# Stick-breaking suffix sums as two fp32r products in place of one fp32 product, in a one-core decoder layer

## The chip, the cores and the metric

The kernel runs on one core of a Trainium2 chip as a single launch. The metric is device time in microseconds (us) of that core. The engines are TensorE (PE, with its weight loads shown apart as PEld), VectorE (DVE), ScalarE (ACT), GpSimd (POOL) and SyncE (SP, which only issues transfers here). Each runs its own list of instructions in order and waits for the others only at semaphores.

## The reference

One decoder layer over 512 tokens of width 1024. The part that matters here is stick-breaking attention, 8 heads of width 64:

```python
z = einsum(q, k) * dh ** -0.5
before = s_pos < t_pos
log_1m = where(before, log_sigmoid(-z), 0)        # = -softplus(z)
csum = cumsum(log_1m, axis=-1)
log_a = log_sigmoid(z) + (csum[..., -1:] - csum)  # a suffix sum over the keys
a = where(before, exp(log_a), 0)
out = a @ v
```

Around it the layer has a combined input projection, a sparse attention whose indexer picks the 128 best keys per query, a gated merge, an output projection, a router, and 16 SwiGLU experts.

## The kernel before

Phases follow one another on PE: input projections (to about 176 us of the profile), stick-breaking attention (to about 288), sparse attention (to about 370), merge and output projection (to about 475), router, experts.

**Stick-breaking steps.** Heads go in 4 pairs (`hp`), key tiles of 128 from the last to the first (`i` = 3, 2, 1, 0). This gives 16 steps `m`, and step `m` handles for two heads the columns `S - 128 i` of all queries at or after key tile `i`: 128, 256, 384, 512 columns per head, so tiles of 256, 512, 768 and 1024 elements per partition. Keys lie on the partitions. A step is made of:

- `z(m)` on PE (L750): the logits into one of two PSUM tiles `zt`, used in turn. It waits until `weights(m - 2)` has read that tile.
- `soft(m)` on ACT (L1203 to L1205): three passes, Abs, Exp, Ln, that leave log(1 + exp(-|z|)).
- `softplus(m)` on DVE (L1566, L1568): adds max(z, 0) and zeroes what isn't `before`.
- `suffix(m)` on PE (L768, L770): adds minus the softplus tiles of this and all later key tiles to `zt`, by products with `negtri` (own tile) and `negones` (later tiles), both 128x128 fp32, then a bf16 product that masks. One step has (4 - i) such fp32 products for each of two heads; 80 in all.
- `weights(m)` on ACT (L1212): Exp of `zt`, the attention weights `ab`.
- `av_a(hp)` on PE (L783), once per pair: weights times values.

**The order.** In turn `m` of the loop PE issues two "triples" of a gate projection (a triple is three fp32r products of 512 columns, L612 to L614, for an fp32 product split in high and low parts), then `z(m+1)`, the index products of the sparse attention (L796), two more triples, at `i` = 3 also `av_a`, then `suffix(m)`. ACT issues `soft(m+1)`, the relu of the index products (L1189), in even turns the copy of a finished gate block (L1227) and after every second of them the rounding of a weight chunk (L1087), then `weights(m)`. DVE issues `softplus(m+1)`, the score sums (L1590, L1592), at turns 4, 8 and 12 the low part of a weight chunk (L1445), then rounds of the top-k search (`topk_rounds`; one round is L1605 and L1606 on a score row). There are 48 rounds, 16 for each of three query tiles with rows of 256, 384 and 512 elements: four rounds a turn at turns 4 to 7, three a turn from turn 8, and the remaining 8 in the sparse phase.

**Sparse phase.** There are 16 units `p`, four for each query tile. DVE takes `rows(p+1)` (L1653), `normal(p)` (L1665), at p = 1, 5, 9, 13 the low part of a weight chunk, then `topk_rounds(2)` as long as rounds remain. PE's `turn(p)` (L868) waits for `normal(p)`. The mask of the third query tile is needed at unit 8, that of the fourth at unit 12.

Of the kernel before, what the change touches and what calls it, by code (L numbers as in the profile page):

```python
# [19 lines left out]
F32 = mybir.dt.float32  # L20
F32R = mybir.dt.float32r
BF16 = mybir.dt.bfloat16
I32 = mybir.dt.int32
ALU = mybir.AluOpType
ACT = mybir.ActivationFunctionType
AX = mybir.AxisListType

P = 128
D = 1024
S = 512  # L30
# [50 lines left out]
def hybrid_layer(nc, x, c, w_ada, b_ada, norm1_g, w_in, q_norm_g, k_norm_g, rel_bias, w_o_a, w_o_b,  # L81
# [9 lines left out]
    def at(name, shape, dt, kb):  # L91
        assert BASE + kb * 1024 + int(np.prod(shape[1:])) * (2 if dt == BF16 else 4) <= 229368
        return nc.alloc_sbuf_tensor_at(name, [P] + shape, dt, offset=BASE + int(kb * 1024))
# [36 lines left out]
    qk_sq = at("qk_sq", [NT, 10, DH], F32, 152)  # L130
    sp_late = [[at(f"sp{i}{b}", [2, S - P * i], F32, 174 + b * 3 + (i == 2)) for b in range(2)] for i in (2, 3)]
    sp_soon = [at(f"sp{i}", [2, S - P * i], F32, 180 + 4 * i) for i in range(2)]
    ab = [at(f"ab{i}", [2, S - P * i], F32, 187 + (0, 4, 7, 9)[i]) for i in range(NT)]
    rel = at("relu_tmp", [2, S], F32, 197)
    lrow = [at(f"lrow{i}", [2, S], F32, 182 + 4 * i) for i in range(2)]
# [37 lines left out]
    def tiny(name, shape, dt=F32):  # L173
        kb = small[0]
        n = int(np.prod(shape)) * (2 if dt == BF16 else 4)
        small[0] = kb + (n + 31) // 32 * 32 / 1024
        return at(name, shape, dt, kb)

    ident = tiny("ident", [P])
    ones = tiny("ones", [P])  # L180
    negones = tiny("negones", [P])
    negtri = tiny("negtri", [P])
    before = tiny("before", [P])
    identb = tiny("identb", [P], BF16)
    neg_ge = tiny("neg_ge", [P], BF16)
# [22 lines left out]
    with ExitStack() as ctx:  # L208
# [5 lines left out]
        def sem(name):  # L214
            return ctx.enter_context(nc.semaphore(name))
# [94 lines left out]
        for n, ch in enumerate(chunks):  # L310
# [24 lines left out]
            sem(n) for n in ("h_ss", "h_sd", "h_rows", "xT_ps", "xT_sb", "hT_hi", "hT_sp"))  # L335
        mod1_ps, mod1_sb, h_full = (sem(n) for n in ("mod1_ps", "mod1_sb", "h_full"))
        qk_var, qk_sd, qk_norm = sem("qk_var"), sem("qk_sd"), sem("qk_norm")
        z_ps, z_soft, sp_ready, s_ps, a_ready = (
            sem(n) for n in ("z_ps", "z_soft", "sp_ready", "s_ps", "a_ready"))
        oa_ps, oa_hi, oa_sp = sem("oa_ps"), sem("oa_hi"), sem("oa_sp")  # L340
        side_ps, side_sb = sem("side_ps"), sem("side_sb")
        score_ok, score_cut = sem("score_ok"), sem("score_cut")
# [56 lines left out]

        def sp_tile(hp, i):  # L400
            return sp_late[i - 2][hp % 2] if i >= 2 else sp_soon[i]


        side_a = [[] for _ in STEPS]
# [87 lines left out]
        def _(pool):  # L492
            n_chain = [0]

            def link(ins):
                n_chain[0] += 1
                ins.then_inc(pool_chain, 1)
                pool.wait_ge(pool_chain, n_chain[0])

            def tri(t, fill, op, base, cm, step):  # L500

                link(pool.affine_select(out=t[:, :], in_=t[:, :], compare_op=op, fill=fill, base=base,
                                        pattern=[[step, P]], channel_multiplier=cm))
# [9 lines left out]
            pool.dma_start(rel_sb[0:BUCKETS, :], rel_bias).then_inc(ld_rel, 16)  # L513
            link(pool.memset(identb[:, :], 0.0))
            tri(identb, 1.0, ALU.not_equal, 0, 1, -1)
            link(pool.memset(negones[:, :], -1.0))
            link(pool.memset(negtri[:, :], -1.0))
            tri(negtri, 0.0, ALU.is_ge, 0, 1, -1)
            link(pool.memset(before[:, :], 1.0))
            tri(before, 0.0, ALU.is_gt, 0, -1, 1)  # L520
            link(pool.memset(neg_ge[:, :], BIG_NEG))
# [84 lines left out]
        def _(pe):  # L606
# [154 lines left out]
            def suffix(m):  # L761

                hp, i = STEPS[m]
                pe.wait_ge(sp_ready, m + 1)
                for r in range(2):
                    for j in range(NT - 1, i - 1, -1):
                        lhs = negtri if j == i else negones
                        pe.matmul(zt[m % 2][:, r, P * (j - i):S - P * i], lhs[:, :], sp_tile(hp, j)[:, r, :],  # L768
                                  start=False, stop=False, skip_group_check=True)
                    last = pe.matmul(zt[m % 2][:, r, 0:P], identb[:, :], neg_ge[:, :], start=False, stop=True,  # L770
                                     skip_group_check=True)
                last.then_inc(s_ps, 1)
# [298 lines left out]
        def _(act):  # L1071
# [7 lines left out]
            def high(n):  # L1079

                w = w_of[n]
                act.wait_ge(raw_in[raw_slot[n]], fill[n])
                if spl_prev[w] is not None:
                    act.wait_ge(*used[spl_prev[w]])
                nk = chunks[n][1]
                top = max(b for _, b, _ in chunks[n][2])
                act.activation(cols(w_hi[spl_slot[w]], 0, top, nk), cols(raw[raw_slot[n]], 0, top, nk), ACT.Copy  # L1087
                               ).then_inc(hi_ready, 1)
# [26 lines left out]
                    act.activation(act_hi[:, k, :], hfull[:, k % 4, :], ACT.Copy).then_inc(hT_hi, 1)  # L1115

            high(next(todo))
            act.wait_ge(xT_ps, 1)
            for k in (6, 1, 2, 3, 4, 5):
                x_copy(k, k)  # L1120
# [74 lines left out]
            def soft(m):  # L1195
# [8 lines left out]
                link(act.activation(t, t, ACT.Exp, scale=-1.0))  # L1204
                act.activation(t, t, ACT.Ln, bias=1.0).then_inc(z_soft, 1)  # L1205

            def weights(m):
                hp, i = STEPS[m]
                act.wait_ge(s_ps, m + 1)
                if hp:  # L1210
                    act.wait_ge(oa_ps, hp)
                act.activation(ab[i][:, :, :], zt[m % 2][:, :, 0:S - P * i], ACT.Exp).then_inc(a_ready, 1)  # L1212
# [16 lines left out]
                        high(next(todo))  # L1229

            soft(0)
            soft(1)
            high(next(todo))
            seg_copy("va", va)
            act.wait_ge(st_mod, 32)
            for m, (hp, i) in enumerate(STEPS):
                if m:
                    gate_rows(FILL_A[m] - 2)
                    if m + 1 < len(STEPS):
                        soft(m + 1)  # L1240
                for t in side_a[m]:
                    side_task(*t)
                gate_rows(FILL_A[m])
                weights(m)
                for t in side_b[m]:
                    side_task(*t)
                if hp and i == 2:
                    oa_high(hp - 1)
# [181 lines left out]
        def _(dve):  # L1430
# [130 lines left out]
            def softplus(m):  # L1561

                hp, i = STEPS[m]
                t = sp_tile(hp, i)
                dve.wait_ge(z_soft, m + 1)
                link(dve.scalar_tensor_tensor(out=t[:, :, :], in0=zt[m % 2][:, :, 0:S - P * i], scalar=0.0, in1=t[:, :, :],  # L1566
                                              op0=ALU.max, op1=ALU.add))
                dve.tensor_tensor(t[:, :, 0:P], t[:, :, 0:P], before[:, :].unsqueeze(1).broadcast_to([P, 2, P]), ALU.mult  # L1568
                                  ).then_inc(sp_ready, 1)

            def oa_low(hp):
# [44 lines left out]
            def gate_splits(triples):  # L1616

                while n_gate[0] < min(triples // 8, 16):
                    b = n_gate[0]
                    n_gate[0] += 1  # L1620
                    if b % 2:
                        raw_chunks(1)

            softplus(0)
            for m, (hp, i) in enumerate(STEPS):
                if m + 1 < len(STEPS):
                    softplus(m + 1)
                if m == 0:
                    raw_chunks(1)
                for t in side_a[m]:  # L1630
                    side_task(*t)
                gate_splits(FILL_A[m])
                topk_rounds(4 if m < 8 else 3)
                for t in side_b[m]:
                    side_task(*t)
                if hp and i == 1:
                    oa_low(hp - 1)
# [313 lines left out]
```

## Time and profile before

| what | value |
|---|---|
| median of 3 runs | 869.4 us (868.77 to 871.4) |
| profiled execution, its own time | 867.77 us |
| its span | 866.0 us |
| PE busy | 807.1 us, 93% |
| DVE busy | 615.7 us, 71% |
| ACT busy | 439.6 us, 51% |
| mean granted TensorE clock | 0.963 of full |

Busy time is what an engine spent in instructions. In the timeline, a row holds a start, a duration, and then what ran; a matmul row's duration reaches from its start to its modelled end, so that rows of pipelined products overlap, and what a product costs is the distance from one start to the next. An fp32 product is recorded as two instructions (x2), an fp32r product as one; both show their type as f32, and the tile names tell which is which.

### The profile page before, as it was taken

To read this page: it belongs to the slowest core of one execution; us is meant where nothing else is said; L and a number is where in the kernel's file an instruction comes from. 1 tells how busy PE (TensorE), PEld (TensorE's weight loads), DVE (VectorE), ACT (ScalarE), POOL (GpSimd) and SP (SyncE) were. 2 spreads that over 40 slices of the span, in tenths; PEclk is the share of its full clock that TensorE was granted. 3 is DMA by queue.
4 is the path that set the end of the run, shared out by engine and by line. 5 is a ranking of instruction groups with operands and counts; after the bars stand their busy time and mean duration, and the time that the engine had idled before them with its cause. 6 is when DMAs were issued, how large, how long until landed. Compare 5 with 4: busy or idle time off the path is not lost.

```text
span 866.0 us, 10677 instructions
## 1 busy us (share of the span) xinstructions
PE 807.1 (93%) x4014; PEld 643.5 (74%) x4014; DVE 615.7 (71%) x786; ACT 439.6 (51%) x519; POOL 73.4 (8%) x67
## 2 busy tenths in 40 slices
PE   3799999999999889999997779999999999999993
PEld 3687687776666556678886777888888888888882
DVE  4676877425998875536655557888888888888882
ACT  6334224465556345563214607575756566665660
POOL 4020000000000000000000000021111111111111
PEclk9799999999999999999999559999999999999997
DMA  8919993111031112051463245899989898989863
GB/s 257 356 33 386 372 363 141 52 47 50 1 98 49 53 49 74 24 213 63 158 249 132 75 152 179 307 313 318 322 313 337 303 337 310 336 305 334 314 230 51
DMA packets 84330, 174.43 MB, mean 201 GB/s; under 512 B 7696, under 2 KB 27256, under 8 KB 82240
## 3 DMA queue, kind: packets, MB, share of 16 engines
q1 hardware_dynamic: 79200, 156.29, 50.7%
q0 software_dynamic: 5088, 17.59, 8.3%
q8 instruction: 25, 0.41, 0.2%
q14 instruction: 17, 0.14, 0.0%
HBM read 163.34 MB, written 10.52 MB: 201 GB/s over the span
## 4 chain that ended last, share of the span: by engine, by line
PE 81%; DVE 8%; ACT 4%; DMA 3%; issue 2%; SPq 1%; POOL 0%; POOLq 0%; DVEq 0%; ACTq 0%
PE ps L612 19%; PE ps L613 18%; PE ps L614 18%; PE ps L971 7%; PE ps L768 4%; DMA raw<-in_w_in 2%; PE ps L750 1%; DVE w_lo L1445 1%; PE ps L852 1%; PE ps L868 1%; PE ps L880 1%; DMA raw<-in_w_ada 1%; DVE accm L1504 1%; PE ps L783 1%; ACT w_hi L1087 1%
## 5 line engine op out<-in xcount | busy, mean ns | idle before, releaser
L1759 DVE TENSOR_TENSOR w_lo<-raw,w_hi 128x2048 fp32r<-128x2048 f32 x96 | 217.1, 2289 | 22.5 <-ACT w_hi L1361 21.9
L1361 ACT ACTIVATE w_hi<-raw 128x2048 fp32r<-128x2048 f32 x96 | 181.8, 1914 | 15.9 <-PE ps L614 15.9
L612 PE MATMUL ps<-act_lo,w_hi 128*128 128x512 f32 x232 | 98.2, 423 | 7.4 <-DVE act_lo L1487 3.2
L612 PE MATMUL ps<-w_lo,hgT_hi 128*128 128x512 f32 x256 | 101.1, 395 | 0.0
L613 PE MATMUL ps<-w_hi,hgT_lo 128*128 128x512 f32 x256 | 99.7, 390 | 0.0
L614 PE MATMUL ps<-w_hi,hgT_hi 128*128 128x512 f32 x256 | 99.7, 389 | 0.0
L1087 ACT ACTIVATE w_hi<-raw 128x2048 fp32r<-128x2048 f32 (+2 forms) x29 | 52.0, 1794 | 79.7 <-DMA raw<-in_w_in 46.1
L614 PE MATMUL ps<-act_hi,w_hi 128*128 128x512 f32 x232 | 91.1, 393 | 0.0
L613 PE MATMUL ps<-act_hi,w_lo 128*128 128x512 f32 x232 | 90.9, 392 | 0.0
L1445 DVE TENSOR_TENSOR w_lo<-raw,w_hi 128x2048 fp32r<-128x2048 f32 (+2 forms) x29 | 62.0, 2145 | 40.2 <-ACT w_hi L1087 40.1
L591 POOL DMA_INDIRECT out<-ys,slot_tok x16 | 49.3, 3082 | 320.0 <-DVE ys L1855 320.0
L612 PEld LDWEIGHTS ps<-act_lo,w_hi 128*128 128x128 f32 x232 | 43.7, 188 | 32.5 <-issue 16.0
L971 PE MATMUL ps<-sel,act_hi 128*128 128x256 f32 x256 | 64.6, 291 | 3.5 <-DVE sel L1836 3.5
L971 PE MATMUL ps<-sel,act_lo 128*128 128x256 f32 x256 | 64.5, 290 | 0.0
L1374 ACT ACTIVATE hgT_hi<-ps 128x512 fp32r<-128x512 f32 x32 | 19.1, 598 | 79.2 <-PE ps L971 79.2
L614 PEld LDWEIGHTS ps<-w_hi,hgT_hi 128*128 128x128 f32 x256 | 48.1, 188 | 10.2
L612 PEld LDWEIGHTS ps<-w_lo,hgT_hi 128*128 128x128 f32 x256 | 48.1, 188 | 9.6
L613 PEld LDWEIGHTS ps<-w_hi,hgT_lo 128*128 128x128 f32 x256 | 48.1, 188 | 9.4
L971 PEld LDWEIGHTS ps<-sel,act_hi 128*128 128x128 f32 x256 | 51.0, 199 | 4.1 <-issue 3.5
L612 PE MATMUL ps<-w_lo,act_hi 128*128 128x512 f32 x128 | 51.8, 405 | 1.3 <-DVE w_lo L1445 1.3
L612 PE MATMUL ps<-w_lo,hidT_hi 128*128 128x512 f32 x128 | 50.0, 390 | 2.9 <-issue 2.9
L971 PEld LDWEIGHTS ps<-sel,act_lo 128*128 128x128 f32 x256 | 51.0, 199 | 0.5
(260 smaller groups left out, 1497.3 us busy)
## 6 DMA issues: line engine op xcount, KB each, us to landing
raw<-in_w_gate SPq DMA_DIRECT2D x32, 1024.0 KB, 8.5
raw<-in_w_up SPq DMA_DIRECT2D x32, 1024.0 KB, 6.4
raw<-in_w_down SPq DMA_DIRECT2D x32, 1024.0 KB, 8.5
raw<-in_w_in SPq DMA_DIRECT2D x16, 1024.0 KB, 6.7
raw<-in_w_ada SPq DMA_DIRECT2D x16, 1024.0 KB, 7.5
raw<-in_w_ada SPq DMA_DIRECT2D x8, 512.0 KB, 7.0
raw_early<-in_w_ada SPq DMA_DIRECT2D x8, 512.0 KB, 6.2
raw<-in_w_out SPq DMA_DIRECT2D x4, 1024.0 KB, 4.9
```

What stands on the lines that cost most here:

```text
L591: pool.indirect_dma_start(out[0], bass.IndirectOffsetOnAxis(slot_tok[:, X % 2:X % 2 + 1], 0), ys[X % 2][:, :], None, compute_op=ALU.add).t ...
L612: pe.matmul(o, a[0], b[1], start=start, stop=False)
L613: pe.matmul(o, a[1], b[0], start=False, stop=False)
L614: return pe.matmul(o, a[0], b[0], start=False, stop=stop)
L750: last = pe.matmul(zt[m % 2][:, r, 0:S - P * i], head(kaT, 2 * hp + r, P * i, P * i + P), head(qaT, 2 * hp + r, P * i, S), start=True, sto ...
L768: pe.matmul(zt[m % 2][:, r, P * (j - i):S - P * i], lhs[:, :], sp_tile(hp, j)[:, r, :], start=False, stop=False, skip_group_check=True)
L971: last = pe.matmul(ps[2 + u % 2][:, 2 * P * (kk % 2):2 * P * (kk % 2) + 2 * P], part[:, tt, P * kk:P * kk + P], sel[:, tt, :, :], start=(t ...
L1087: act.activation(cols(w_hi[spl_slot[w]], 0, top, nk), cols(raw[raw_slot[n]], 0, top, nk), ACT.Copy).then_inc(hi_ready, 1)
L1361: act.activation(e_hi[s_][:, :], e_raw[r][:, :], ACT.Copy).then_inc(e_top, 1)
L1374: act.activation(hgT_hi[:, :, 2 * u:2 * u + 2, :].rearrange("p b k s -> p k b s"), ps[2 + u % 2][:, :].rearrange("p (k b s) -> p k b s", k ...
L1445: dve.tensor_tensor(lo, r, hi.bitcast(F32), ALU.subtract).then_inc(chunk_split, 1)
L1759: dve.tensor_tensor(e_lo[s_][:, :], e_raw[r][:, :], e_hi[s_][:, :].bitcast(F32), ALU.subtract).then_inc(e_split, 1)
```

## The change

Each softplus tile is now split in a rounded high part (`sph`, fp32r, written by ACT) and the remainder (`spl`, fp32r, written by DVE over the tile itself), and `suffix` takes two fp32r products where it had one fp32 product. `negones` and `negtri` become fp32r and are rounded once at the start by ACT. ACT gets `split_high(m+1)` ahead of `weights(m)`. DVE gets `split_low(m+1)` ahead of the weight chunk's low part and of the rounds, and issues two rounds a turn instead of three from turn 8 on.

```diff
@@ tensor
             def suffix(m):
                 hp, i = STEPS[m]
+                if m == 0:
+                    pe.wait_ge(neg_ok, 2)
                 pe.wait_ge(sp_ready, m + 1)
                 for r in range(2):
                     for j in range(NT - 1, i - 1, -1):
                         lhs = negtri if j == i else negones
-                        pe.matmul(zt[m % 2][:, r, P * (j - i):S - P * i], lhs[:, :], sp_tile(hp, j)[:, r, :],
-                                  start=False, stop=False, skip_group_check=True)
+                        for part in sp_parts(hp, j):
+                            pe.matmul(zt[m % 2][:, r, P * (j - i):S - P * i], lhs[:, :], part[:, r, :],
+                                      start=False, stop=False, skip_group_check=True)
@@ scalar
+            act.wait_ge(const_ready, 1)
+            act.activation(negones[:, :], negones_f[:, :], ACT.Copy).then_inc(neg_ok, 1)
+            act.activation(negtri[:, :], negtri_f[:, :], ACT.Copy).then_inc(neg_ok, 1)
...
+            def split_high(m):
+                hp, i = STEPS[m]
+                act.wait_ge(sp_full, m + 1)
+                act.activation(sp_parts(hp, i)[0][:, :, :], sp_tile(hp, i)[:, :, :], ACT.Copy).then_inc(sp_hi, 1)
...
             soft(0)
+            split_high(0)
             soft(1)
...
                 gate_rows(FILL_A[m])
+                if m + 1 < len(STEPS):
+                    split_high(m + 1)
                 weights(m)
@@ vector
                 dve.tensor_tensor(t[:, :, 0:P], t[:, :, 0:P], before[:, :].unsqueeze(1).broadcast_to([P, 2, P]), ALU.mult
+                                  ).then_inc(sp_full, 1)
+
+            def split_low(m):
+                hp, i = STEPS[m]
+                hi, lo = sp_parts(hp, i)
+                dve.wait_ge(sp_hi, m + 1)
+                dve.tensor_tensor(lo[:, :, :], sp_tile(hp, i)[:, :, :], hi[:, :, :].bitcast(F32), ALU.subtract
                                   ).then_inc(sp_ready, 1)
...
                 for t in side_a[m]:
                     side_task(*t)
+                if m + 1 < len(STEPS):
+                    split_low(m + 1)
                 gate_splits(FILL_A[m])
-                topk_rounds(4 if m < 8 else 3)
+                topk_rounds(4 if m < 8 else 2)
```

ACT's list of the kernel before, turns 9 and 10: from `soft(10)` to `weights(10)` (`ab_106` and `ab_105` are the weights of steps 9 and 10, `sp_103` and `sp_102` the softplus tiles of 10 and 11).

```order
L1203 ACTIVATE sp_103<-ps 128x768
L1204 ACTIVATE sp_103<-sp_103 128x768
L1205 ACTIVATE sp_103<-sp_103 128x768
L1189 ACTIVATE relu_tmp<-ps 128x1024
L1212 ACTIVATE ab_106<-ps 128x512
L1216 ACTIVATE oaT_hi<-ps 128x512
L1203 ACTIVATE sp_102<-ps 128x1024
L1204 ACTIVATE sp_102<-sp_102 128x1024
L1205 ACTIVATE sp_102<-sp_102 128x1024
L1189 ACTIVATE relu_tmp<-ps 128x1024
L1227 ACTIVATE gate_a<-ps 128x512
L1212 ACTIVATE ab_105<-ps 128x768
```

The same place of ACT in the changed kernel (`ab_120` and `ab_119` are the same weights, `sph` the high parts).

```order
L1219 ACTIVATE sp_103<-ps 128x768
L1220 ACTIVATE sp_103<-sp_103 128x768
L1221 ACTIVATE sp_103<-sp_103 128x768
L1205 ACTIVATE relu_tmp<-ps 128x1024
L1226 ACTIVATE sph_109<-sp_103 128x768
L1233 ACTIVATE ab_120<-ps 128x512
L1237 ACTIVATE oaT_hi<-ps 128x512
L1219 ACTIVATE sp_102<-ps 128x1024
L1220 ACTIVATE sp_102<-sp_102 128x1024
L1221 ACTIVATE sp_102<-sp_102 128x1024
L1205 ACTIVATE relu_tmp<-ps 128x1024
L1248 ACTIVATE gate_a<-ps 128x512
```

A high part now stands between each relu and the weights, and it waits for DVE's softplus of the same turn.

DVE's list of the kernel before, turn 8 and the start of turn 9: from the softplus of step 9 (`sp_98`) to that of step 10 (`sp_103`).

```order
L1566 SCALAR_TENSOR_TENSOR sp_98<-ps,sp_98 128x512
L1568 TENSOR_TENSOR sp_98<-sp_98,before 128x2x128
L1592 SCALAR_TENSOR_TENSOR score_71<-relu_tmp,wi,score_71 128x384 x2
L1445 TENSOR_TENSOR w_lo_59<-raw_50,w_hi_56 128x2048
L1605 MAX m_0_168<-score_71 128x8
L1606 MATCH_REPLACE score_71<-m_0_168,score_71 128x384
L1605 MAX m_1_169<-score_71 128x8
L1606 MATCH_REPLACE score_71<-m_1_169,score_71 128x384
L1605 MAX m_0_168<-score_71 128x8
L1606 MATCH_REPLACE score_71<-m_0_168,score_71 128x384
L1566 SCALAR_TENSOR_TENSOR sp_103<-ps,sp_103 128x768
```

The same place of DVE in the changed kernel.

```order
L1590 SCALAR_TENSOR_TENSOR sp_98<-ps,sp_98 128x512
L1592 TENSOR_TENSOR sp_98<-sp_98,before 128x2x128
L1623 SCALAR_TENSOR_TENSOR score_71<-relu_tmp,wi,score_71 128x384 x2
L1599 TENSOR_TENSOR spl_110<-sp_98,sph_104 128x512
L1469 TENSOR_TENSOR w_lo_59<-raw_50,w_hi_56 128x2048
L1636 MAX m_0_182<-score_71 128x8
L1637 MATCH_REPLACE score_71<-m_0_182,score_71 128x384
L1636 MAX m_1_183<-score_71 128x8
L1637 MATCH_REPLACE score_71<-m_1_183,score_71 128x384
L1590 SCALAR_TENSOR_TENSOR sp_103<-ps,sp_103 128x768
```

A low part has come in ahead of the weight chunk, and one round of three has gone. Over turns 8 to 15 that takes 8 rounds out of this phase; 16 instead of 8 are left for the sparse phase, all on rows of 512 elements, so that they last to unit 7 instead of unit 3.

## Rows read from the trace of the kernel before

**Rows 1.** The page, section 4: the chain that ended last, by engine.

```profile
PE 81%; DVE 8%; ACT 4%; DMA 3%; issue 2%; SPq 1%; POOL 0%; POOLq 0%; DVEq 0%; ACTq 0%
```

**Rows 2.** Windows: busy PE, PEld, DVE, ACT, POOL (instructions), clock, DMA share, GB/s.

```profile
225.00:250.00 25.00, 25.00 (x122) 15.72 (x121) 22.97 (x51) 14.93 (x19) 1.09 (x2) 1.00 0.29 85
```

**Rows 3.** Waits of PE, 155 to 400 us: total, times, longest.

```profile
PE ps L868 <- DVE lrow L1665: 4.2, 3, 2.8
```

**Rows 4.** Timeline of PE: `z(9)` to `z(13)`, and one head of `suffix(11)`.

```profile
230.95 0.70 PE L750 MATMUL ps<-qaT,kaT 64*128 64x256 f32 x4
238.37 0.92 PE L750 MATMUL ps<-qaT,kaT 64*128 64x384 f32 x4
244.59 1.13 PE L750 MATMUL ps<-qaT,kaT 64*128 64x512 f32 x4
252.31 0.49 PE L750 MATMUL ps<-qaT,kaT 64*128 64x128 f32 x4
...
255.10 1.46 PE L768 MATMUL ps<-sp,negones 128*128 128x128 f32 x6
...
257.26 0.22 PE L770 MATMUL ps<-neg_ge,identb 128*128 128x128 bf16 x1
...
261.12 0.70 PE L750 MATMUL ps<-qaT,kaT 64*128 64x256 f32 x4
```

**Rows 5.** Timeline of PE: neighbouring fp32r products of 136, 512 and 256 columns.

```profile
66.53 0.27 PE L704 MATMUL ps<-w_hi,act_lo 128*128 128x136 f32 x1
66.64 0.28 PE L705 MATMUL ps<-w_hi,act_hi 128*128 128x136 f32 x1
...
601.16 0.39 PE L614 MATMUL ps<-w_hi,hgT_hi 128*128 128x512 f32 x1
601.39 0.39 PE L612 MATMUL ps<-w_lo,hgT_hi 128*128 128x512 f32 x1
...
809.85 0.28 PE L971 MATMUL ps<-sel,act_lo 128*128 128x256 f32 x1
809.97 0.28 PE L971 MATMUL ps<-sel,act_hi 128*128 128x256 f32 x1
```

**Rows 6.** Timeline of ACT and DVE in turns 7 to 10.

```profile
229.62 1.03 ACT L1212 ACTIVATE ab<-ps 128x1024 f32<-128x1024 f32 x1 [4.74 <-PE ps L770]
237.04 0.38 ACT L1212 ACTIVATE ab<-ps 128x256 f32<-128x256 f32 x1 [0.43 <-PE ps L770]
238.92 0.55 DVE L1605 MAX8 m<-score 128x8 f32<-128x384 f32 x1
242.67 0.96 DVE L1566 SCALAR_TENSOR_TENSOR sp<-ps,sp 128x768 f32<-128x768 f32 x1
243.66 0.42 DVE L1568 TENSOR_TENSOR sp<-sp,before 128x256 f32<-128x256 f32 x1
245.77 1.02 ACT L1203 ACTIVATE sp<-ps 128x1024 f32<-128x1024 f32 x1 [1.42 <-PE ps L750]
247.92 1.06 ACT L1205 ACTIVATE sp<-sp 128x1024 f32<-128x1024 f32 x1
```

**Rows 7.** Timeline of DVE in turns 4 and 5: four rounds of 256 elements.

```profile
209.39 0.42 DVE L1605 MAX8 m<-score 128x8 f32<-128x256 f32 x1
...
213.33 0.96 DVE L1566 SCALAR_TENSOR_TENSOR sp<-ps,sp 128x768 f32<-128x768 f32 x1
```

**Rows 8.** Timeline of DVE in the sparse phase: rounds of 512 elements, `normal(4)`, a weight chunk.

```profile
301.31 0.69 DVE L1605 MAX8 m<-score 128x8 f32<-128x512 f32 x1
302.81 0.69 DVE L1605 MAX8 m<-score 128x8 f32<-128x512 f32 x1
...
314.26 0.69 DVE L1665 TENSOR_TENSOR lrow<-lrow,rsum 128x512 f32<-128x512 f32 x1
320.49 2.29 DVE L1445 TENSOR_TENSOR w_lo<-raw,w_hi 128x2048 fp32r<-128x2048 f32 x1 [2.25 <-ACT w_hi L1087]
```

**Rows 9.** Timeline of PE: `turn(6)`.

```profile
324.65 0.66 PE L868 MATMUL ps<-ident,lrow 128*128 128x128 f32 x4
```

More of the change, by code:

```diff
@@ L132, in hybrid_layer @@
     sp_soon = [at(f"sp{i}", [2, S - P * i], F32, 180 + 4 * i) for i in range(2)]
+    sph_late = [[at(f"sph{i}{b}", [2, S - P * i], F32R, 201 if (i, b) == (3, 0) else 64 + b * 3 + (i == 2)) for b in range(2)] for i in (2, 3)]
+    sph_soon = [at(f"sph{i}", [2, S - P * i], F32R, 70 + 4 * i) for i in range(2)]
+    spl_late = [[at(f"spl{i}{b}", [2, S - P * i], F32R, 174 + b * 3 + (i == 2)) for b in range(2)] for i in (2, 3)]
+    spl_soon = [at(f"spl{i}", [2, S - P * i], F32R, 180 + 4 * i) for i in range(2)]
+    negones_f = at("negones_f", [P], F32, 135.5)
+    negtri_f = at("negtri_f", [P], F32, 131.5)
     ab = [at(f"ab{i}", [2, S - P * i], F32, 187 + (0, 4, 7, 9)[i]) for i in range(NT)]
@@ L180, in hybrid_layer @@
     ones = tiny("ones", [P])
-    negones = tiny("negones", [P])
-    negtri = tiny("negtri", [P])
+    negones = tiny("negones", [P], F32R)
+    negtri = tiny("negtri", [P], F32R)
     before = tiny("before", [P])
@@ L337, in hybrid_layer @@
         qk_var, qk_sd, qk_norm = sem("qk_var"), sem("qk_sd"), sem("qk_norm")
-        z_ps, z_soft, sp_ready, s_ps, a_ready = (
-            sem(n) for n in ("z_ps", "z_soft", "sp_ready", "s_ps", "a_ready"))
+        z_ps, z_soft, sp_full, sp_hi, sp_ready, s_ps, a_ready = (
+            sem(n) for n in ("z_ps", "z_soft", "sp_full", "sp_hi", "sp_ready", "s_ps", "a_ready"))
+        neg_ok = sem("neg_rounded")
         oa_ps, oa_hi, oa_sp = sem("oa_ps"), sem("oa_hi"), sem("oa_sp")
@@ L401, in sp_tile, with sp_parts @@
             return sp_late[i - 2][hp % 2] if i >= 2 else sp_soon[i]
+        def sp_parts(hp, i):
+            return ((sph_late[i - 2][hp % 2], spl_late[i - 2][hp % 2]) if i >= 2 else (sph_soon[i], spl_soon[i]))
         side_a = [[] for _ in STEPS]
@@ L515, in _ @@
             tri(identb, 1.0, ALU.not_equal, 0, 1, -1)
-            link(pool.memset(negones[:, :], -1.0))
-            link(pool.memset(negtri[:, :], -1.0))
-            tri(negtri, 0.0, ALU.is_ge, 0, 1, -1)
+            link(pool.memset(negones_f[:, :], -1.0))
+            link(pool.memset(negtri_f[:, :], -1.0))
+            tri(negtri_f, 0.0, ALU.is_ge, 0, 1, -1)
             link(pool.memset(before[:, :], 1.0))
@@ L1624, in _ @@
             softplus(0)
+            split_low(0)
             for m, (hp, i) in enumerate(STEPS):
```

## The prediction

> **What bounds the kernel now.** I read the chain of waits by engine first: PE has 81% of it [rows 1], so a microsecond taken from PE counts, if PE doesn't then wait. Next the table of windows. In 25 us of the stick-breaking phase PE is busy all the time and at full clock, but DVE too is busy for 22.97 of the 25 us [rows 2]: whatever is added there meets an engine with 8% of slack. PE's waits come third: from 155 to 400 us the largest entry is 4.2 us in three waits for DVE's `normal` in the sparse phase, the longest 2.8 us [rows 3]. So the attention phases are PE-bound, with DVE close behind, and the chain z, soft, softplus, suffix is hidden by issuing z one turn ahead. Last, the timeline of one pair of heads, which gives all prices below.
>
> **What the change takes from PE.** One head of `suffix(11)` has products of 128, 256, 384 and 512 columns, 1280 in all, from 255.10 to 257.26: 2.16 us, or 1.69 ns a column; 0.22, 0.43, 0.65 and 0.86 us apiece [rows 4]. Neighbouring fp32r products stand 0.11 us apart at 136 columns, 0.12 at 256 and 0.23 at 512 [rows 5]. For 384 no row exists; it lies between 0.12 and 0.23, and I take 0.175. Two of them cost 0.22, 0.24, 0.35 and 0.46: nothing gained at 128, then 0.19, 0.30 and 0.40. The counts are 32, 24, 16 and 8 products, so the gain is 4.6 + 4.8 + 3.2 = 12.6 us, 3.1 us a pair of heads: nothing in `suffix` of i = 3, 0.4 us at i = 2, 1.0 at i = 1, 1.8 at i = 0. With 384 columns at its ends the sum is 10.8 to 14.4 us.
>
> The Trainium skill ("TensorE: Matmul & The Clock Gate", section "Wait — 56ns, not 53.3ns?") states a start to start of N / 2.4 GHz plus some 2.5 ns, 56 ns at 128 columns. By that the 32 narrow products would give 3.4 us more. The trace has 0.11 us at 136 columns with a new fp32r weight load for each, so here the measured pace decides.
>
> **What it adds.** ACT gets 16 high parts. Its pass over 1024 elements takes 1.06 us, over 256 elements 0.38 [rows 6], so 0.38, 0.6, 0.83 and 1.06 us: 2.9 us a pair. DVE gets 16 low parts, a subtraction of two tiles: 0.96 us at 768 elements and 0.42 at 256 [rows 6], so 0.42, 0.69, 0.96 and 1.22, 3.3 us a pair. DVE loses one round of three from turn 8 on; three rounds of 384 elements run from 238.92 to 242.67, 1.25 us each [rows 6]. The two roundings of `negones` and `negtri` at the start cost ACT some 0.6 us, in the stretch where it waits for the first transposes; I take 0, at most 0.6.
>
> More matters where the new pieces stand. The high part waits for DVE's softplus, and `weights(m)` is queued behind it on ACT, and `z(m+2)` on PE waits for `weights(m)`. Before, ACT could do the weights right after its own soft passes. Now there is one loop through three engines in every turn: z, three ACT passes, softplus, high part, weights of the step before, next z.
>
> **The loop in turns 8 to 11, by rows.** After z(9) at 230.95 ACT does what it did. The low part of the weight chunk, 2.29 us on DVE [rows 8], ended where the rounds began, 238.92 [rows 6], so it began at 236.6, right behind the chunk's high part on ACT. There the new high part now comes next and takes ACT to 237.2, the low part DVE to 238.0, the weight chunk to 240.2, two rounds to 242.7. That is the very moment at which softplus(10) started before [rows 6]: the round taken out is spent.
> - z(10) starts at 238.37 as before. softplus(10) takes 0.96 + 0.42 us to 244.1, the high part, with 0.1 us for each crossing, to 245.05, weights(9) 0.6 to 245.65. From the end of the weights to z it takes 0.3 us (229.62 + 1.03 to 230.95) [rows 4, 6]. z(11) starts at 245.95. Before it was 244.59; PE's own work would allow 244.2. PE waits 1.75 us.
> - z(11): first ACT pass 1.18 us later, Ln over at +4.39 [rows 4, 6], softplus 1.7 us, high part 1.06, weights(10) 0.81, crossings 0.5: z(12) at +8.4 us. Own work is 7.72 - 0.96 = 6.76 [rows 4]. PE waits 1.65 us.
> - z(12) and z(9) are narrow; their loops need about 5 and 7 us, and PE's own work is 7.05 and 7.4: no wait.
>
> So the pair takes 7.4 + 7.6 + 8.4 + 7.05 = 30.45 us against 30.17 before (230.95 to 261.12) [rows 4]: +0.3 us. Of 3.1 us gained, all are waited away.
>
> **The other pairs.** The first has no rounds; only the loop itself binds, 6.9 us at 768 elements and 8.4 at 1024. I take a net -1.0 us. The second keeps four rounds of 256 elements, 3.94 us (209.39 to 213.33) [rows 7] where the third has 2.5, and nothing was taken out: softplus of the 768-element tile comes 1.4 us later than in the walk above, and the turn after the 1024-element tile loses 0.7 us too. Net +2.7 us. The fourth has no index products from its second turn on, so PE's own work is shorter there and the wait longer, by an estimated 0.9 us; against that the last suffix gains 1.8 us with nobody to wait for. Net +0.7 us. The phase: -1.0 + 2.7 + 0.3 + 0.7 = +2.7 us.
>
> **The rounds that move.** Eight rounds of 512 elements, 1.5 us each (301.31 to 302.81) [rows 8], now run in units 4 to 7. normal(4) ends at 314.95; two rounds go to 317.95, then rows(6) and normal(5), under 1.9 us by the stretch priced below, to 319.8, before the chunk that came at 320.49: in time. The weight chunk ends at 322.78 as before [rows 8]; two rounds go to 325.8. From the chunk's end to turn(6) it took 324.65 - 322.78 = 1.87 us [rows 8, 9], so turn(6) comes at 327.65: +3.0 us. The two units after it have no chunk, and PE is then 3 us late itself: nothing more, at most 1 us. If PE arrives earlier, the wait is longer by as much.
>
> **Sum.** +2.7 + 3.0 = +5.7 us, on the profiled execution's own 867.77: 873.5 us. The median stands 1.6 us above that execution, so 869.4 + 5.7 = 875.1, rounded 875. What follows is PE-bound or fed by transfers that start when buffers come free, so it moves as a whole.
>
> The bounds of what no row shows: the crossing from DVE to ACT in the middle of the loop, which I took as 0.1 us, between 0 and 0.3 for about eight turns that bind: -0.8 to +1.6 us. The fp32r pace at 384 columns hardly matters where PE waits: 0.5 us either way. The first and second pair by 1.5 us each.
>
> **The rivals.**
> - *PE stays the bound (faster).* The loop is shorter than I add it up or is absorbed by the two narrow turns, as it would be if weights were not held up behind the high part. Then the phase gives its 12.6 us and the sparse phase takes back 3.0: 860 us. With half the waits it is 866. Against it speaks that the third pair's walk uses only measured starts, and that DVE is at 92%. It decides for faster if the waits of the wide turns stay under about 2.3 us a pair instead of 3.4 to 5.8. Chance 0.17, for both together.
> - *The moved rounds are hidden.* The phase loses 2.7 us and the sparse phase nothing, because DVE stood idle there, 2.25 us ahead of the chunk alone [rows 8]. Near 872. Chance 0.15, in part within the 0.3%.
> - *The clock falls.* In the trace the longest wait in this stretch, 2.8 us, left the clock full [rows 2, 3]; new waits are 3 us and more. If the grant went to 1.2 GHz after one of them and stayed so for 10 us, 5 us more: 881. Chance 0.08. The Trainium skill ("TensorE: Matmul & The Clock Gate", section "HAM oscillation — how this bites in real kernels") warns that idle gaps re-throttle the array; no row of this phase shows it.
> - *Forecast:* waits in both phases, 875. Chance 0.60, its own range 871 to 879.
>
> All in all the range is 865 to 881. A measurement of this kernel can tell 0.3%, 2.6 us, from no change. Faster 0.17; the same 0.12 (most of it from the second rival and the forecast's lower end); slower 0.71.
>
> **What would show it.** Right: `L768` without x2 pairs, half the busy time of `suffix`; PE waiting for ACT's `ab` before z, 1.5 to 3.5 us in each turn of a 768- or 1024-element tile, none before narrow ones, some 15 us in all; z(9) to z(13) at 30 us or a little more; a wait of about 3 us more before turn(6). Wrong: PE busy throughout from 176 to 285 us with the phase some 12 us shorter; or softplus starting right behind Ln in the wide turns of pairs two and three; or fp32r pairs of 256 columns at 0.4 us.

## The result and the profile after

| what | kernel before | changed kernel |
|---|---|---|
| median (17 runs each) | 870.7 us (867.04 to 875.75) | 876.07 us (872.87 to 879.68) |
| ratio | | 1.0065, 95% interval 1.0045 to 1.0084 |
| profiled execution, its span | 866.0 us | 872.2 us |
| PE busy | 807.1 us | 802.0 us |
| DVE busy | 615.7 us | 627.3 us |
| ACT busy | 439.6 us | 449.5 us |
| mean granted clock | 0.963 | 0.956 |

The changed kernel is slower by 0.65%, 5.7 us. PE has 5 us less to do, and the span is 6.2 us longer. The chain that ended last shows where the path went; it answers to [rows 1].

```profile
PE 70%; DVE 15%; ACT 7%; DMA 3%; issue 3%; SPq 1%; POOL 0%; POOLq 0%; DVEq 0%; ACTq 0%
```

DVE's share of the path has gone from 8% to 15%, ACT's from 4% to 7%, PE's from 81% to 70%.

I follow the time by three marks on PE: `z(0)`, the first logits of the sparse phase (`logits(0)`), and the first product of the output projection (`oa0`). "Stick phase" is from the first to the second, "sparse phase" from the second to the third.

| | before | after | difference |
|---|---|---|---|
| z(0) to z(5) | 37.78 | 36.47 | -1.31 |
| z(5) to z(9) | 29.31 | 31.86 | +2.55 |
| z(9) to z(13) | 30.17 | 30.08 | -0.09 |
| z(13) to logits(0) | 26.87 | 27.70 | +0.83 |
| stick phase | 124.13 | 126.11 | +1.98 |
| sparse phase | 94.49 | 98.72 | +4.23 |

The rest cancels out: z(0) comes 0.8 us earlier, and what follows `oa0` takes 0.8 us more. The difference of the spans, 6.2 us, is that of the last two rows.

The windows of the changed kernel, with the columns of [rows 2] (busy PE, PEld, DVE, ACT, POOL with their instructions, clock, DMA share, GB/s):

```profile
225.00:250.00 25.00, 22.86 (x121) 14.93 (x119) 23.41 (x53) 16.13 (x23) 1.48 (x2) 1.00 0.28 85
176.00:286.00 110.00, 100.49 (x527) 67.60 (x527) 81.09 (x160) 72.17 (x100) 2.05 (x4) 0.97 0.13 41
213.00:221.00 8.00, 5.83 (x23) 3.33 (x23) 6.69 (x18) 5.56 (x8) 0.00 (x0) 0.79 0.01 2
305.00:313.00 8.00, 6.33 (x24) 3.92 (x25) 7.66 (x24) 3.17 (x12) 0.00 (x0) 0.79 0.27 97
```

PE was busy for all of the first window before; now it stands idle for 2.14 of 25 us. In the long window it is idle for 9.51 us; the same stretch of the kernel before is this row, idle 0.08:

```profile
176.00:286.00 110.00, 109.92 (x542) 72.23 (x540) 81.10 (x172) 63.79 (x86) 1.66 (x4) 1.00 0.13 39
```

The last two windows of the changed kernel show what was not there before: the granted clock falls to half (1.2 GHz). A mean of 0.79 over 8 us is 3.4 us at half. It happens at 215 and 307 us, in these two windows, and at 277 us:

```profile
274.00:282.00 8.00, 6.01 (x25) 3.92 (x25) 4.94 (x10) 5.44 (x7) 0.00 (x0) 0.79 0.17 59
```

PE's waits from 155 to 400 us, the view of [rows 3] (total, times, longest):

```profile
PE ps L760 <- ACT ab L1233: 8.6, 7, 2.8
PE ps L881 <- DVE lrow L1699: 7.1, 4, 3.2
PE ps L622 <- ACT gate_a L1248: 1.1, 2, 0.7
```

`L760` is z and `L1233` the weights: PE waits before z for the weights of the step two before it (`z(7)` for `weights(5)`), seven times, where before it never did. `L881` is `turn`, 4.2 us before and 7.1 now.

The third pair's z, then one head of `suffix(11)`; it answers to [rows 4]:

```profile
238.75 0.92 PE L760 MATMUL ps<-qaT,kaT 64*128 64x384 f32 x4
246.39 1.13 PE L760 MATMUL ps<-qaT,kaT 64*128 64x512 f32 x4 [1.70 <-ACT ab L1233]
254.41 0.49 PE L760 MATMUL ps<-qaT,kaT 64*128 64x128 f32 x4 [0.55 <-ACT ab L1233]
257.19 0.22 PE L781 MATMUL ps<-sph,negones 128*128 128x128 f32 x1
...
257.64 0.34 PE L781 MATMUL ps<-sph,negones 128*128 128x384 f32 x1
257.82 0.34 PE L781 MATMUL ps<-spl,negones 128*128 128x384 f32 x1
258.00 0.39 PE L781 MATMUL ps<-sph,negtri 128*128 128x512 f32 x1
258.23 0.40 PE L781 MATMUL ps<-spl,negtri 128*128 128x512 f32 x1
258.47 0.23 PE L783 MATMUL ps<-neg_ge,identb 128*128 128x128 bf16 x1
261.47 0.70 PE L760 MATMUL ps<-qaT,kaT 64*128 64x256 f32 x4
```

One head takes 1.28 us (257.19 to 258.47) where it took 2.16: the products are as cheap as forecast (1.27), and z(11) and z(12) wait all the same.

Why z waits is seen in turn 5 of ACT and DVE and the start of turn 6 of PE; the same kind of rows as [rows 6]. The softplus and the high part are those of step 6, the weights those of step 5, and z is z(7):

```profile
212.33 0.96 DVE L1590 SCALAR_TENSOR_TENSOR sp<-ps,sp 128x768 f32<-128x768 f32 x1
213.33 0.42 DVE L1592 TENSOR_TENSOR sp<-sp,before 128x256 f32<-128x256 f32 x1
...
213.78 0.84 ACT L1226 ACTIVATE sph<-sp 128x768 fp32r<-128x768 f32 x1 [2.89 <-DVE sp L1592]
...
214.53 0.58 ACT L1233 ACTIVATE ab<-ps 128x512 f32<-128x512 f32 x1
...
215.17 1.98 PE L760 MATMUL ps<-qaT,kaT 64*128 64x512 f32 x4 [2.77 <-ACT ab L1233]
```

DVE comes to softplus at 212.33 only, out of its rounds. ACT has stood for 2.89 us before the high part; the weights, which need nothing of it, stand behind it; and z(7) waits 2.77 us for them. z(7) itself then takes 1.98 us instead of 1.13, at half the clock.

In the sparse phase, the answer to [rows 8, 9]:

```profile
322.38 2.29 DVE L1469 TENSOR_TENSOR w_lo<-raw,w_hi 128x2048 fp32r<-128x2048 f32 x1 [1.88 <-ACT w_hi L1100]
324.59 0.69 DVE L1636 MAX8 m<-score 128x8 f32<-128x512 f32 x1
...
328.84 0.69 DVE L1699 TENSOR_TENSOR lrow<-lrow,rsum 128x512 f32<-128x512 f32 x1
...
329.59 0.66 PE L881 MATMUL ps<-ident,lrow 128*128 128x128 f32 x4 [3.20 <-DVE lrow L1699]
```

The two moved rounds stand between the chunk and unit 6, and turn(6) waits 3.20 us.

### The profile page after: what moved, and what is told of

It reads as the page before. It is cut to its first block, busy times and chain, and to the rows that moved or that the text cites. A ratio compares the mean times of both kernels' runs of the same rounds, so it can differ in the third digit from the quotient of the medians.

```text
span 872.2 us, 10717 instructions
## 1 busy us (share of the span) xinstructions
PE 802.0 (92%) x4012; PEld 642.3 (74%) x4014; DVE 627.3 (72%) x802; ACT 449.5 (52%) x537; POOL 73.9 (8%) x67
## 4 chain that ended last, share of the span: by engine, by line
PE 70%; DVE 15%; ACT 7%; DMA 3%; issue 3%; SPq 1%; POOL 0%; POOLq 0%; DVEq 0%; ACTq 0%
PE ps L622 18%; PE ps L624 17%; PE ps L623 17%; PE ps L984 7%; DVE w_lo L1469 2%; DVE score L1637 2%; DMA raw<-in_w_in 2%; DVE m L1636 1%; DVE acc L1479 1%; ACT w_hi L1100 1%; PE ps L760 1%; PE ps L865 1%; PE ps L781 1%; DVE sp L1590 1%; PE ps L881 1%
## 5 line engine op out<-in xcount | busy, mean ns | idle before, releaser
L624 PEld LDWEIGHTS ps<-act_hi,w_hi 128*128 128x128 f32 x232 | 44.3, 191 | 10.0
```

The lines of the kernel that those rows point to most:

```text
L624: return pe.matmul(o, a[0], b[0], start=False, stop=stop)
```

## The experiments

Each was timed in five rounds beside the kernel before. "Order" is the theory of the forecast: the weights, queued behind a high part that itself waits for DVE, close a loop through three engines; and the rounds that move make turn(6) late. Its rival is that DVE (or ACT) simply has too much to do. The times of the two phases are of one trace each, and some of these traces hold stretches at half clock; the ratios are of 6 to 17 runs.

| kernel | ratio to before, 95% | median us | stick phase | sparse phase |
|---|---|---|---|---|
| changed | 1.0065 (1.0045 to 1.0084) | 876.07 | 126.11 | 98.72 |
| e1 weights first | 1.0016 (0.9994 to 1.0039) | 872.59 | 123.89 | 98.63 |
| e2 three rounds | 1.0082 (1.0055 to 1.0109) | 878.67 | 129.65 | 98.14 |
| e3 gain alone | 0.9922 (0.9899 to 0.9946) | 864.2 | 116.13 | 96.64 |
| e4 cost alone | 1.0109 (1.0078 to 1.0141) | 880.05 | 135.41 | 95.04 |
| e5 before, two rounds | 1.0049 (1.0019 to 1.0079) | 875.66 | 124.13 | 102.01 |
| e6 filler | 1.0069 (1.0044 to 1.0093) | 876.11 | 125.73 | 99.86 |
| e7 order and rounds | 0.9989 (0.9966 to 1.0012) | 868.75 | 121.82 | 96.09 |
| e8 before, spread | 0.995 (0.9925 to 0.9975) | 865.5 | 124.14 | 90.98 |
| e9 round between | 0.9916 (0.9887 to 0.9945) | 861.04 | 118.23 | 91.48 |
| e10 low first | 0.9923 (0.9898 to 0.9948) | 861.99 | 118.70 | 92.88 |
| e11 swap and spread | 0.9962 (0.9935 to 0.999) | 866.57 | 122.29 | 93.09 |

**e1, weights ahead of the high part.**

```diff
-                if m + 1 < len(STEPS):
-                    split_high(m + 1)
                 weights(m)
+                if m + 1 < len(STEPS):
+                    split_high(m + 1)
```

> The changed kernel with one swap on ScalarE: weights(m) ahead of split_high(m+1). Theory (the weights are held up behind a high part that waits for VectorE): z no longer waits long in the wide turns; from z(2) to the first logits the phase gets some 4 to 5 us shorter than in the changed kernel (109.8 to 111.8 less that), time near 871. Rival (VectorE has simply too much work, wherever the high part stands): the phase stays within 1 us of the changed kernel and the time at 876, since VectorE's work is the same. The sparse phase still loses some 3 us before turn(6) by either.

Measured: 1.0016, and in the trace no wait of z for the weights any more. PE's waits in the same view:

```profile
PE ps L622 <- ACT gate_a L1248: 4.8, 4, 1.6
PE ps L781 <- DVE spl L1599: 2.1, 3, 0.8
```

Two neighbouring calls in ACT's list are worth 0.5% of the kernel, and 872.59 us is near what the theory gave. The phase moved less than it gave: from z(2) to the first logits it takes 109.57 us in this trace, where the changed kernel takes 111.80, so 2.2 us less and not 4 to 5. It is only 0.24 us shorter than before the change: what was a wait at z is in good part now one at the gate copy (also behind the high part) and at the suffix. The first entry holds 0.7 us of the sparse phase, which the kernel before waits there too.

**e2, the rounds back in the stick phase.**

```diff
-                topk_rounds(4 if m < 8 else 2)
+                topk_rounds(4 if m < 8 else 3)
```

> The changed kernel with three rounds a turn from turn 8 on, as before the change. Theory: each wide turn of pairs three and four starts its softplus 1.25 us later, so the stick-breaking phase grows by some 3 us or a little more, and the sparse phase loses its extra 3 us before turn(6) again: the time stays at 875 to 877. If the moved rounds were the whole cost of the change, the time would fall by 3 us to 873 and the stick-breaking phase would not grow.

Measured: stick phase +3.54 us over the changed kernel, as the theory gave; time 878.67, above its 875 to 877; and this wait before z in place of 8.6:

```profile
PE ps L760 <- ACT ab L1233: 11.9, 8, 3.6
```

The sparse phase was to give back 3 us and gave 0.58. The wait at turn(6) did go: turn(6) stands 4.45 us after turn(5), 7.49 in the changed kernel. But turn(0) waits 2.41 us here instead of 0.89, and the clock falls at 303 us, right behind that wait, and once more at 316 us. So the round taken out of each turn does help the loop, by more than it costs in the sparse phase in this pair of traces; the ratios of the two kernels have overlapping intervals (medians 2.6 us apart).

**e3, the gain alone.** Both products read one tile that DVE writes; no splits.

```diff
-                        for part in sp_parts(hp, j):
+                        for part in (sp_parts(hp, j)[1],) * 2:
...
-                if m + 1 < len(STEPS):
-                    split_high(m + 1)
...
-                if m + 1 < len(STEPS):
-                    split_low(m + 1)
...
-                topk_rounds(4 if m < 8 else 2)
+                topk_rounds(4 if m < 8 else 3)
```

> Two fp32r products a tile, but no high and low parts: the softplus is written once as fp32r by VectorE, and both products read it (so each sum is counted twice, and the output is another). Three rounds a turn as before. Theory: TensorE gives its 12.6 us less what the old loop through ScalarE and VectorE then binds; I add up some 6 us of waits, so 6 to 12 us faster than before, 859 to 865, and no change in the sparse phase. If the fp32r products gave nothing (rival), it would stand at 870.

Measured: 0.9922, stick phase 8.00 us shorter than before, at full clock. Its waits between z(0) and the first logits are these:

```profile
PE ps L781 <- DVE spl L1590: 2.2, 2, 1.4
PE ps L622 <- ACT gate_a L1248: 0.9, 2, 0.4
```

8.0 plus these 3.1 is 11.1 us, which is the forecast's 12.6 for what PE is spared, less 1.5.

**e4, the cost alone.** The splits stay; one fp32 product of the high part is taken, the remainder left out.

```diff
-                        for part in sp_parts(hp, j):
-                            pe.matmul(..., lhs[:, :], part[:, r, :],
+                        for part in sp_parts(hp, j)[:1]:
+                            pe.matmul(..., lhs[:, :], part[:, r, :].bitcast(F32),
```

(and `negones`, `negtri` in fp32, three rounds as in e2)

> The high and low parts on ScalarE and VectorE with their waits as in the changed kernel, three rounds a turn as before the change, but one fp32 product of the high part alone in place of the two fp32r products (so the remainder is left out of the sums). Theory: the loop binds in the wide turns and TensorE gives nothing back, so slower than before by 8 to 14 us, 879 to 885, all of it in the stick-breaking phase. If the additions were hidden by themselves (rival), within 2 us of before.

Measured: 1.0109; the stick phase is 11.28 us longer than before with PE's products as they were, two dips of the clock among it. The splits, placed as they are, cost more than the 8.0 us that the products give in e3. The two don't add up to e2 (3.3 against 5.5 us): waits and the clock are not additive.

**e5, the kernel before with two rounds a turn.**

```diff
-                topk_rounds(4 if m < 8 else 3)
+                topk_rounds(4 if m < 8 else 2)
```

> The kernel before the change with two rounds a turn from turn 8 on, so that 16 rounds instead of 8 are left for the sparse phase, and nothing else. Theory: TensorE was the bound of the stick-breaking phase, so that phase keeps its 124.1 us from z(0) to the first logits, and the sparse phase loses some 3 us at turn(6): 3 us slower than before. If the moved rounds are hidden by gaps on VectorE (rival), no change.

Measured: stick phase the same to 0.01 us (DVE's slack there was not needed), sparse phase +7.52 us, time +0.49%, 4.3 us. The wait entry of the sparse phase is 6.9 us where it was 4.2 [rows 3]; the longest is again 3.2. The rest is clock:

```profile
304.00:312.00 8.00, 6.74 (x21) 3.80 (x22) 7.66 (x25) 3.13 (x12) 0.00 (x0) 0.57 0.22 77
326.00:338.00 12.00, 8.83 (x34) 5.25 (x34) 10.89 (x29) 3.90 (x12) 0.00 (x0) 0.72 0.24 84
```

So the moved rounds cost 2.7 us of wait, near the 3 us of the forecast, and the other 4.8 us of this trace go with two stretches of low clock. Over 11 runs they cost 4.3 us, and the mean granted clock of these is 0.956 where the kernel before has 0.959 (32 runs).

**e6, a filler.** 34 bf16 products into an unused part of a bank ahead of z(7), so that PE is at work where it waited.

```diff
+                if m == 6:
+                    pe.wait_ge(side_sb, n_side[0])
+                    for _ in range(34):
+                        pe.matmul(ps[6][:, 384:512], identb[:, :], neg_ge[:, :], ...)
                 if 1 <= m < len(STEPS) - 1:
                     z(m + 1)
```

> The changed kernel with 34 small bf16 products into an unused part of a PSUM bank, some 1.9 us, ahead of z(7), where TensorE waited 2.8 us for the weights and its clock then fell to 1.2 GHz for about 4 us (z(7) took 1.98 us instead of 1.13). Theory (the clock falls because TensorE idles): the wait shrinks to under 1 us, the clock stays full there, z(7) takes 1.1 us, and the phase gets 0.8 to 1.5 us shorter. Rival (the clock falls for another reason, or the loop does not feel it): z(7) at 1.98 us still, or the phase no shorter. The whole time moves by less than this comparison can tell.

```profile
213.69 2.07 PE L847 MATMUL ps<-neg_ge,identb 128*128 128x128 bf16 x34
216.63 1.13 PE L760 MATMUL ps<-qaT,kaT 64*128 64x512 f32 x4 [0.87 <-ACT ab L1238]
```

z(7) comes as late as before, 8.50 us after z(6) in both, but takes 1.13 us instead of 1.98, and z(8) follows after 8.03 us instead of 8.86: 0.83 us for the dip at that place. The whole phase gained only 0.38, because in this run z(15) fell into half the clock for its full length (1.98 us against 1.49). No difference in the timing (1.0069). The direction was right, the effect on the phase half of the least I had expected. That the filler is what kept the clock up at z(7) is not shown by one trace: the last section has two executions of one list of which one dips and the other doesn't.

**e7, order and rounds together.** e1, the low part behind the weight chunk's, and the rounds spread by hand.

```diff
-                if m + 1 < len(STEPS):
-                    split_low(m + 1)
                 gate_splits(FILL_A[m])
+                if m + 1 < len(STEPS):
+                    split_low(m + 1)
-                topk_rounds(4 if m < 8 else 2)
+                topk_rounds([0, 0, 0, 0, 2, 4, 5, 5, 1, 2, 3, 2, 1, 2, 3, 2][m])
...
-                topk_rounds(2)
+                topk_rounds([2, 0, 2, 2, 2, 1, 2, 2, 2, 1, 0, 0, 0, 0, 0, 0][p])
```

> The changed kernel with weights(m) ahead of split_high(m+1), the low part of the softplus behind that of the weight chunk, the rounds spread as 2, 4, 5, 5, then 1, 2, 3, 2 twice over turns 4 to 15 (few ahead of a wide softplus), and 2, 0, 2, 2, 2, 1, 2, 2, 2, 1 over units 0 to 9 of the sparse phase. Theory: no round delays a wide softplus, and no unit has both a weight chunk and two rounds; the stick-breaking phase 2 to 4 us shorter than with the swap alone (123.9), the sparse phase (98.6 with the swap alone) 5 to 7 us shorter. Time 861 to 866, 5 to 10 us faster than before the change. If VectorE's total work were the bound, it would stand where the swap alone does, near 872.

Measured: 868.75, a miss by 3 us, and not distinguishable from the kernel before. The trace shows two places. In the stick phase a low part now stands behind 2.29 us of chunk (first row), and after that wait the clock is at half for 6.8 us (0.72 over 12 us); with 121.82 us the phase still is where I had it, 2.1 us under e1's. The miss is in the sparse phase, 2.5 us under e1's instead of 5 to 7: turn(6) and turn(10) wait 1.7 and 1.8 us (second row). Both follow a unit with a weight chunk and one round, so that not even one round has room beside a chunk.

```profile
PE ps L781 <- DVE spl L1599: 3.8, 2, 3.1
PE ps L881 <- DVE lrow L1699: 4.4, 3, 1.8
236.00:248.00 12.00, 8.90 (x31) 5.66 (x30) 10.46 (x18) 6.85 (x10) 3.08 (x2) 0.72 0.50 175
```

**e8, the kernel before with the eight sparse rounds spread.**

```diff
-                topk_rounds(2)
+                topk_rounds((2, 0, 2, 2, 2)[p] if p < 5 else 0)
```

> The kernel before the change with its 8 rounds of the sparse phase spread as 2, 0, 2, 2, 2 over units 0 to 4 instead of 2, 2, 2, 2. Theory: the 2.8 us wait ahead of turn(2) is two rounds and a weight chunk in one unit; without the rounds it goes, 2 to 3 us faster than before. So much of the gain of the combined kernel has nothing to do with fp32r. Rival: the wait is the chunk's alone, no change.

Measured: 0.995, 4.4 us, more than the 2 to 3 expected. The wait of 2.8 us at turn(2) is gone and the sparse phase is 3.51 us shorter; the mean granted clock of its 10 runs is 0.962 against 0.959. This has nothing to do with the fp32r products; it is the bar that a version with them has to pass.

**e9, e10, e11: the splits and the rounds placed by what each engine waits for.** All three have e1's order. e9 has one round ahead of the low part, in the time in which DVE waited for the high part:

```diff
+            ROUNDS_A = (0, 0, 0, 0, 3, 4, 4, 2, 3, 2, 1, 3, 2, 3, 4, 2)
+            ROUNDS_B = (3, 0, 1, 2, 3, 0, 2, 2, 2, 0, 0, 0, 0, 0, 0, 0)
...
+                ahead = min(1, ROUNDS_A[m])
+                topk_rounds(ahead)
                 if m + 1 < len(STEPS):
                     split_low(m + 1)
                 gate_splits(FILL_A[m])
-                topk_rounds(4 if m < 8 else 2)
+                topk_rounds(ROUNDS_A[m] - ahead)
...
-                topk_rounds(2)
+                topk_rounds(ROUNDS_B[p])
```

> The changed kernel with weights(m) ahead of split_high(m+1), one round ahead of split_low(m+1), and the 48 rounds spread as 3,4,4,2,3,2,1,3,2,3,4,2 over turns 4 to 15 and 3,0,1,2,3,0,2,2,2 over units 0 to 8. The loop theory says: the round fills the time in which DVE waited for the high part, so that the suffix is not late and neither are the weights or z; the phase from z(0) to the first sparse logits takes 118 to 121 us (116.1 was reached with no splits at all), the sparse phase to the first product of oa0 91 to 94 us, and the time is 860 to 864 us, below the 865.5 of the kernel before with its eight sparse rounds spread. The rival, that DVE is simply full in this phase (its busy time is what counts, not its order), says 121.5 us and more for the phase and 866 to 869 us.

e10 has no round ahead, and the counts 1, 4, 5, 4, 2, 3, 3, 2, 0, 2, 3, 3 (from turn 4) and 3, 0, 1, 2, 3, 0, 2, 2, 3:

> As the run with a round between, but split_low(m+1) ahead of the rounds as in the changed kernel, the rounds spread as 1,4,5,4,2,3,3,2,0,2,3,3 and 3,0,1,2,3,0,2,2,3. Weights still stand ahead of split_high. The loop theory expects the phase at 119 to 122 us and the time at 861 to 865 us; DVE-is-full expects the same as for the run with a round between, 866 to 869.

e11 keeps the changed kernel's turns (four rounds, then two) and spreads only the sparse ones:

> The changed kernel with weights(m) ahead of split_high(m+1), turns as changed (four rounds, then two), and only the sixteen sparse rounds spread as 3,0,2,2,2,1,2,2,2 over units 0 to 8 instead of two a unit over units 0 to 7. If order and rounds add up from the runs so far: 872.6 of the swapped kernel, less the wait at turn(2) and the wait at turn(6) and what they cost the clock, 5 to 7 us by the difference that the spread made to the kernel before (5.0 us) : 866 to 868 us, phase 123.9 us as with the swap alone, sparse phase 92 to 94. If the sparse waits were not the cause of the low clock there, the gain is under 3 us: 870.

Measured: 861.04, 861.99 and 866.57 us, each inside what the order theory gave; the rival's 866 to 869 us for e9 and e10 is out. The stick phases of e10 and e11 came out 0.3 and 1.6 us shorter than I had written; for e11 that is the clock, below. e9 and e10 can't be told apart, so a gain of the round ahead of the low part itself is not shown. Both leave units 1 and 5, which have a chunk, without a round. In e9 `weights(5)` no longer stands behind the high part, and z(7) has no wait at all:

```profile
209.29 0.60 ACT L1233 ACTIVATE ab<-ps 128x512 f32<-128x512 f32 x1
209.42 0.96 DVE L1590 SCALAR_TENSOR_TENSOR sp<-ps,sp 128x768 f32<-128x768 f32 x1
...
210.62 1.13 PE L760 MATMUL ps<-qaT,kaT 64*128 64x512 f32 x4
...
210.88 0.84 ACT L1226 ACTIVATE sph<-sp 128x768 fp32r<-128x768 f32 x1 [0.99 <-DVE sp L1592]
```

and DVE does more work in the same stretch, 83.20 us between 176 and 280 us where the changed kernel has 77.22, so that it was not full. The granted clock is 1.00 throughout (the columns are those of [rows 2]):

```profile
176.00:280.00 104.00, 99.22 (x534) 66.43 (x533) 83.20 (x167) 72.56 (x99) 2.18 (x5) 1.00 0.13 41
```

e9 is the best version: 0.84% below the kernel before (0.55 to 1.13%). It keeps all of the arithmetic. Against e8, with a ratio of 0.995, it is ahead by 0.3%; the intervals overlap and the two were timed beside different runs, so that the fp32r products are worth something over e8 is likely, not shown; nor was the kernel before run with e9's rounds. One trace of each says 5.4 us, stick phase 118.23 against 124.14 us, sparse phase 91.48 against 90.98, but e9's is its fastest run, 3.5 us under its median, and e8's is 2.5 us above its own.

## Why the prediction was right

The forecast was +5.7 us and 875; measured were 1.0065, +5.7 us, and 876.07, inside the likeliest case's own range. What makes the kernel slower is what the forecast said: waits of z for the weights, and turn(6). That the number fits so closely is in part luck: the waits of the stick phase were smaller than forecast, and a clock that the sum held at full made up for it.

- *Gain on PE, 12.6 us.* One head of `suffix(11)` takes 1.28 us against 1.27 forecast, and 384 columns stand at 0.18 us, where I had taken 0.175 between two rows. The pair of 256 columns costs 0.28 and not 0.24, and the first narrow pair 0.17 and not 0.22. e3 returns 11.1 of 12.6 as time or as named waits.
- *The loop eats the gain in the wide turns.* Pair by pair I had -1.0, +2.7, +0.3, +0.7; measured -1.31, +2.55, -0.09, +0.83. The second and the fourth hold a dip of the clock each; e6, without the one at z(7), has +1.70 for the second pair (31.01 us from z(5) to z(9)). For the third pair the four distances were 7.4, 7.6, 8.4 and 7.05; they are 7.36, 7.64, 8.02 and 7.06. The cause is shown by e1: with the weights ahead of the high part z doesn't wait. The crossing that I had taken as 0.1 us, DVE to ACT, is not seen larger: the high part starts at 213.78 after a pass that starts at 213.33 and lasts 0.42.
- *The size of the waits* was a miss. I wrote some 15 us in all, 1.5 to 3.5 in each turn of a wide tile; PE stands idle for 9.5 us, 8.6 of it before z, and only z(7), z(11) and z(15) wait that long (2.77, 1.70 and 1.99). The clock was at half for 3.4 us twice in the phase (0.97 over 110 us is 3.3 us of clock), which lengthens work instead of showing as a wait. And I had looked only before z: of the 1.65 us forecast ahead of z(12), 0.55 stands there and 0.43 before the gate products of the same turn. The distances between marks were near, and how much of them would show as a wait was not. Nor is it only the 768- and 1024-element turns: z(12), z(8) and z(4) are narrow and wait 0.5 to 0.6 us each.
- *The moved rounds, +3.0 us.* turn(6) waits 3.20 us. The sparse phase is 4.23 us longer; the 1.2 us beyond the forecast are the clock at 307 us, which made turn(2) to turn(3) 1.5 us longer (306.59 to 313.02 against 305.43 to 310.39), less a little that later units took back. e5 has both parts apart from the splits: a wait of 3.2 us at turn(6), and dips.
- *The rivals.* PE bound and faster would have needed the order of e1 and the rounds of e9. The rounds hidden: no, by e5. The clock: it did fall, for which I had 0.08, in three dips of 3.4 us. e6 prices the one at z(7) at 0.83 us, the one at 307 us is worth up to the 1.5 us above, and the one at 277 us has no run of its own; 3.4 us at half can cost at most 1.7. So by estimate the changed kernel's stick phase would at full clock be between 0.6 us shorter and 1.2 us longer than before, where the forecast had +2.7. More runs say the same. The mean granted clock is 0.955 over the 17 runs of the changed kernel and 0.959 over the 22 of the kernel before that were timed beside e1 to e4. The share withheld times the time is 39.6 and 35.4 us, so that by estimate at most some 4 of the 5.7 us are the clock. This rival came true beside the forecast, at less than its 5 us, and its 0.08 was too low. Nor did the rows that I leaned on bear on it: the window of [rows 2] ends at 250 us, and the wait of 2.8 us is at 303 to 305.

What the forecast did not see is how close a better version was: two calls exchanged and the rounds dealt out otherwise turn +0.65% into -0.84%.

## What to carry to other kernels

When a cheaper product needs a new pass on another engine, look first at what stands behind that pass in its engine's list: here the weights, which did not need it, waited for it and carried the wait to PE. An engine that was busy for 92% of a window had no room here for a new pass where it stood, and had it a few instructions away. Work that is due later can go into the time in which that engine waits for the new pass, as in e9, though e9 gains nothing clear over e10 by it. Price both sides by themselves (the gain without its cost, the cost without its gain) before the whole is judged. And look at the clock too: a new wait can cost more than its own length.

## What the runs showed of the hardware

**The clock falls after waits of 1.6 to 2.8 us in one execution and not in another.** Before, PE waits 2.8 us at turn(2) at full clock [rows 3]; in the changed kernel the same wait of 2.79 us before turn(2) is followed by the row at 305 us with 0.79. This is the kernel before in the same place, its wait ending at 305.43:

```profile
305.00:313.00 8.00, 7.47 (x39) 4.88 (x40) 7.69 (x20) 3.60 (x14) 0.00 (x0) 1.00 0.12 43
```

The strongest case is e1 beside e11, whose lists are the same to the end of the stick phase. This is e1 around step 7:

```profile
216.00:224.00 8.00, 6.42 (x29) 4.10 (x28) 7.62 (x18) 6.34 (x10) 0.00 (x0) 0.79 0.00 0
```

and this e11, 6.2 us later, as z(0) comes 6.2 us later there:

```profile
222.20:230.20 8.00, 6.41 (x36) 4.27 (x36) 7.62 (x18) 6.67 (x10) 0.00 (x0) 1.00 0.00 0
```

PE is busy for the same time in both, but gets through 29 products at 0.79 of the clock and through 36 at all of it. The two waits before it are the same too, 0.84 and 1.57 us in e1, 0.83 and 1.59 in e11. e1 has two such dips in the phase and e11 none, and e11's stick phase is 1.60 us shorter, 122.29 against 123.89. So some 1.6 us of a difference between two single traces of these kernels can be the clock. The ratios average over that, and still hold what one kernel's clock is lower by on the whole. What makes the grant fall in one run and not in another stays open. The Trainium skill ("TensorE: Matmul & The Clock Gate", section "HAM oscillation — how this bites in real kernels") says that idle gaps re-throttle the array; dips do follow waits here, but not each wait.

**fp32r products of 128 columns save next to nothing over fp32.** In `suffix(11)` a pair takes 0.17 us for one head and 0.26 for the other, where one fp32 product takes 0.22, while at 512 columns the pair takes 0.47 instead of 0.86.
